# A two-model forward pass on one core: eight swaps in the mixers' list, and another head, hand-over and tail

## The reference

```python
def first_block(x, ...):                      # two blocks
    for l in range(2):
        h = rms_norm(x, norm_mix[l])
        if l == 0: x = x + pool_attn_mixer(h, ...)   # 4 pooled groups and 8 attention heads, then pa_w_out
        else:      x = x + rglru_mixer(h, ...)       # gated linear recurrence, then rg_w_out
        x = x + conv_ffn(rms_norm(x, norm_ffn[l]), ...)
    return x

def second_block(x, c, ...):                  # one block
    sh1, sc1, gt1, sh2, sc2, gt2 = jnp.split(silu(c) @ ada_w[l] + ada_b[l], 6)
    p = (rms_norm_2(x, norm_mix_g[l]) * (1.0 + sc1) + sh1) @ w_in[l]
    y_a = rwkv7_mixer(p[..., :OFF_B], ...)    # the recurrence: state (state*w + sa b + v k) over positions
    y_b = spatial_gating_mixer(...); y_c = short_conv_mixer(...)
    y_d = s5_mixer(p[..., OFF_D:OFF_G], ...)  # complex diagonal state space, scans over positions
    gates = jax.nn.sigmoid(p[..., OFF_G:])
    x = x + gt1 * ((gates[0] * y_a + gates[1] * y_b + gates[2] * y_c + gates[3] * y_d) @ w_o[l])
    x = x + gt2 * (square(relu(h2 @ ffn_w1[l])) @ ffn_w2[l])
    return rms_norm_2(x, final_g)
```

## Time and profile before

| | us |
|---|---|
| median of 3 runs | 1149.91 |
| lowest and highest run | 1147.52, 1151.16 |
| the profiled execution's own time | 1149.63 |
| its span in the trace | 1147.8 |
| TensorE busy in it | 1087.0 |

### The profile page before, as it was taken

The page is one execution under the profiler, slowest core; times in us unless marked ns, Lnnn a source line. Parts: engine busy times, 40 slices in busy tenths (PEclk is TensorE's granted clock), DMA queues, the critical chain, the costliest instruction groups (busy, mean ns, idle before and its releaser), DMA issues.

```text
span 1147.8 us, 21003 instructions
## 1 busy us (share of the span) xinstructions
PE 1087.0 (95%) x8588; PEld 1032.6 (90%) x8588; DVE 835.6 (73%) x1444; ACT 641.7 (56%) x1098; POOL 67.2 (6%) x79
## 2 busy tenths in 40 slices
PE   6996999999998969999999999999999999999996
PEld 6874999999997859999999988899989989999996
DVE  6464898887886387987787778998875587655452
ACT  7544676665565786656555685322233368875340
POOL 1231200000102001000000000000000011000010
PEclk9998999999999979999999999999999999999998
DMA  9366365556665845676776553222335275556651
GB/s 341 116 202 230 132 210 182 185 171 183 190 199 194 276 149 166 214 235 216 239 235 183 191 170 106 88 84 90 121 105 154 70 252 181 184 179 182 182 159 37
DMA packets 59856, 200.41 MB, mean 175 GB/s; under 512 B 6768, under 2 KB 11504, under 8 KB 59632
## 3 DMA queue, kind: packets, MB, share of 16 engines
q1 hardware_dynamic: 58032, 194.54, 52.7%
q10 hardware_dynamic: 1728, 4.53, 1.1%
HBM read 197.99 MB, written 1.05 MB: 173 GB/s over the span
## 4 chain that ended last, share of the span: by engine, by line
PE 81%; DVE 10%; ACT 5%; DMA 2%; issue 1%; ACTq 0%; SPq 0%; POOL 0%; DVEq 0%
PE ps L472 81%; DVE wlo L1556 2%; ACT whi L1039 1%; DVE xr L1562 1%; DMA ring<-pa_w_out 1%; ACT L1039 1%; DMA ring<-pa_w_in 1%; ACT xr L1039 1%; ACT rr L1039 0%; DMA ring<-w_o 0%; DVE rst L1585 0%; DVE raw L1556 0%; DVE bks L1556 0%; DVE hl L1556 0%; ACT sc L1039 0%
## 5 line engine op out<-in xcount | busy, mean ns | idle before, releaser
L472 PE MATMUL ps<-hh,whi 128*128 128x256 f32 (+1 forms) x1656 | 481.2, 291 | 18.0 <-DVE wlo L1556 15.5
L472 PE MATMUL ps<-hh,wlo 128*128 128x256 f32 (+1 forms) x1656 | 471.1, 284 | 0.0
L472 PE MATMUL ps<-hl,whi 128*128 128x256 f32 (+1 forms) x1656 | 469.1, 283 | 0.0
L1556 DVE TENSOR_TENSOR wlo<-ring,whi 128x1024 fp32r<-128x1024 f32 (+1 forms) x313 | 376.1, 1216 | 70.6 <-ACT whi L1039 69.9
L1039 ACT ACTIVATE whi<-ring 128x1024 fp32r<-128x1024 f32 (+1 forms) x313 | 321.7, 1039 | 72.4 <-PE ps L472 52.4
L472 PEld LDWEIGHTS ps<-hh,whi 128*128 128x128 f32 x1656 | 316.2, 191 | 38.8 <-issue 31.0
L472 PEld LDWEIGHTS ps<-hl,whi 128*128 128x128 f32 x1656 | 316.9, 191 | 1.6 <-issue 1.2
L472 PEld LDWEIGHTS ps<-hh,wlo 128*128 128x128 f32 x1656 | 316.4, 191 | 0.0
L472 PE MATMUL ps<-hidh,whi 128*128 128x256 f32 x608 | 172.2, 283 | 0.0
L472 PE MATMUL ps<-hidh,wlo 128*128 128x256 f32 x608 | 172.1, 283 | 0.0
L472 PE MATMUL ps<-hidl,whi 128*128 128x256 f32 x608 | 172.0, 283 | 0.0
(11 more groups left out here) (360 smaller groups left out, 1345.6 us busy)
## 6 DMA issues: line engine op xcount, KB each, us to landing
ring<-ffn_w_in SPq DMA_DIRECT2D x88, 512.0 KB, 4.1
ring<-ffn_w SPq DMA_DIRECT2D x64, 512.0 KB, 4.1
ring<-w_in SPq DMA_DIRECT2D x51, 512.0 KB, 3.4
ring<-ada_w SPq DMA_DIRECT2D x48, 512.0 KB, 4.3
ring<-ffn_w_out SPq DMA_DIRECT2D x32, 448.0 KB, 3.4
ring<-rg_w_in SPq DMA_DIRECT2D x20, 512.0 KB, 4.3
ring<-pa_w_in SPq DMA_DIRECT2D x16, 512.0 KB, 7.4
ring<-ffn_w_out SPq DMA_DIRECT2D x16, 512.0 KB, 3.6
```

What stands on the lines that cost most here:

```text
L472: return e.matmul(o, l, r, start=start, stop=stop)
L1556: return e.tensor_tensor(o, a, b, op)
```

## The change

Four edits stand in it. In the head, ten matmuls of a buffer of zeros are put in front on TensorE, which no longer waits there for the constants; chunk 0 lands and is split in two halves, each with its own signal; the two larger of ACT's three DMAs are issued behind chunk 0. At the end of the attention stage, the eighth A moves to the end of ATTN, its chunks ahead of pa_w_out's, pa_w_out reads its inputs in the order 4, 5, 6, 3, 2, 7, 1, 0, and `mod_turn` is called behind column 2 only. In PLAN, eight pairs "S", "R" become "R", "S". In the tail, four DMAs of two tiles replace eight of one.

```diff
 ATTN = [ ...
-    ("A",), 0, ("T", 7), ("O", 2), ("G", 3), ("A",), ("G", 2), ("A",), ("O", 3), ("G", 1), ("A",), ("G", 0),
+    ("A",), 0, ("T", 7), ("O", 2), ("G", 3), ("A",), ("G", 2), ("A",), ("O", 3), ("G", 1), ("A",), ("G", 0), ("A",),
 ]
@@ weight_order
     for m in range(8):
         whole("pa_w_out", 8, (m,))
-        if m == 1:
-            columns()
@@ PLAN (one of its lines; eight such pairs in all)
-    "R", (0, 0), "S", "R", (1, 0), "R", (2, 0), "S", "R", (0, 3), "R", (1, 3), "R", (2, 3), "R", (3, 3), "R", (4, 3),
+    "R", (0, 0), "R", "S", (1, 0), "R", (2, 0), "R", "S", (0, 3), "R", (1, 3), "R", (2, 3), "R", (3, 3), "R", (4, 3),
@@ tensor_program, linear(..., rows=range(8))
-                    for q in range(n):
+                    for i, q in enumerate(rows[0:n]):
...
-                            low.wait_ge(e, c)
+                            low.wait_ge(e, c if c or q > 3 else "half")
@@ tensor_program, row_stats
                     p = take(("stat", 0))
+                    ones_in.wait_ge(e, "all")
@@ tensor_program, pool_attn
                 def also(m):
-                    mod_turn()
-                    if m == 0:
-                        mod_step()
-                residual(1, "pa_w_out", 8, ..., also)
+                    if m == 2:
+                        mod_turn()
+                residual(1, "pa_w_out", 8, ..., also, (4, 5, 6, 3, 2, 7, 1, 0))
@@ tensor_program, start
-            ones_in.wait_ge(e, "all")
+            at_dve.wait_ge(e, "zeros")
+            for i in range(10):
+                mm(ps[7][:, 0:T], raw[0][:, 0:128], raw[0], True, True)
@@ scalar_program, feed (DVE's feed splits chunk 0 in the same way)
+                        if n == 0:
+                            act(whi[0][:, 0:4, :], ring[0][:, 0:4, :], ACT.Copy).then_inc(*high.up("half"))
+                            landed_late.wait_ge(e, "all")
+                        k = 0 if n else 4
+                        act(whi[j % NS][:, k:nk, :], ring[n % NR][:, k:nk, :], ACT.Copy).then_inc(*high.up(n))
@@ scalar_program, start
-            e.dma_start(cst[:, 0:384], d["cst"][:, 0:384]).then_inc(*ones_in.up("all", 16))
-            e.dma_start(vec[:, 32:], d["vec"][:, 32:]).then_inc(*vecs_in.up("all", 16))
...
                 if m == 3:
                     feed(-1 - AHEAD)
+                    e.dma_start(cst[:, 0:384], d["cst"][:, 0:384]).then_inc(*ones_in.up("all", 16))
+                    e.dma_start(vec[:, 32:], d["vec"][:, 32:]).then_inc(*vecs_in.up("all", 16))
@@ sync_program
+                if n == 0:
+                    e.dma_start(dst[:, 0:4, :], src[:, 0:4, :]).then_inc(*landed[0].up(0, 16))
+                    e.dma_start(dst[:, 4:, :], src[:, 4:, :]).then_inc(*landed_late.up("all", 16))
...
-            for m in range(8):
-                fin.wait_ge(e, m)
-                e.dma_start(out[:, m, :], x[:, m, :]).then_inc(*x_out.up("all", 16))
+            for m in (0, 2, 4, 6):
+                fin.wait_ge(e, m + 1)
+                e.dma_start(out[:, m:m + 2, :], x[:, m:m + 2, :]).then_inc(*x_out.up("all", 16))
```

More of the change, by code:

```diff
@@ L491, in give, with linear @@
                 freed[b] = s, ev
-            def linear(w, ms, of, nk, need):
+            def linear(w, ms, of, nk, need, rows=range(8)):
                 outs = [take((w, m))[:, 0:T] for m in ms]
@@ L500, in linear @@
                         for (c, _, _), o in zip(parts, outs):
-                            low.wait_ge(e, c)
+                            low.wait_ge(e, c if c or q > 3 else "half")
                             j = turn[c] % NS
-                            mm(o, whi[j][:, q, :], rh, k + q == 0, False)
+                            mm(o, whi[j][:, q, :], rh, k + i == 0, False)
                             mm(o, whi[j][:, q, :], rl, False, False)
-                            t = mm(o, wlo[c % NR][:, q, :], rh, False, k + q == nk - 1)
-                            if q == n - 1:
+                            t = mm(o, wlo[c % NR][:, q, :], rh, False, k + i == nk - 1)
+                            if i == n - 1:
                                 t.then_inc(*through.up(c))
@@ L538, in stats, with residual @@
                 give(("stat", n), mean, n)
-            def residual(n, w, nk, of, need, also=None):
+            def residual(n, w, nk, of, need, also=None, rows=range(8)):
                 for ms in ([0, 1], [2], [3], [4], [5], [6], [7]) if nk == 8 else [[m] for m in range(8)]:
-                    linear(w, ms, of, nk, need)
+                    linear(w, ms, of, nk, need, rows)
                     for m in ms:
@@ L679, in also @@
                 def also(m):
-                    mod_turn()
-                    if m == 0:
-                        mod_step()
-                residual(1, "pa_w_out", 8, pair(pah, pal), lambda k: at_dve.wait_ge(e, ("pal", k)), also)
+                    if m == 2:
+                        mod_turn()
+                residual(1, "pa_w_out", 8, pair(pah, pal), lambda k: at_dve.wait_ge(e, ("pal", k)), also, (4, 5, 6, 3, 2, 7, 1, 0))
             def conv_ffn(l):
@@ L1050, in feed @@
                             used(e, at_turn[j - NS])
-                        act(whi[j % NS][:, 0:nk, :], ring[n % NR][:, 0:nk, :], ACT.Copy).then_inc(*high.up(n))
+                        if n == 0:
[3 more added lines that the diff above has]
+                        act(whi[j % NS][:, k:nk, :], ring[n % NR][:, k:nk, :], ACT.Copy).then_inc(*high.up(n))
             def out_of(w, m, nk=8):
@@ L1218, in pool_attn @@
                         part[at[0]](*at[1:])
-                def also(m):
-                    next(steps, None)
-                    if m == 0:
-                        mod_step()
-                residual(1, "pa_w_out", 8, also)
+                residual(1, "pa_w_out", 8, lambda m: next(steps, None))
             def conv_ffn(l):
@@ L1573, in feed @@
                         nk, j = order[n][3], n % NR
+                        if n == 0:
+                            high.wait_ge(e, "half")
+                            low_of(wlo[0][:, 0:4, :], ring[0][:, 0:4, :], whi[0][:, 0:4, :]).then_inc(*low.up("half"))
+                        k = 0 if n else 4
                         high.wait_ge(e, n)
-                        low_of(wlo[j][:, 0:nk, :], ring[j][:, 0:nk, :], whi[turn[n] % NS][:, 0:nk, :]).then_inc(*low.up(n))
+                        low_of(wlo[j][:, k:nk, :], ring[j][:, k:nk, :], whi[turn[n] % NS][:, k:nk, :]).then_inc(*low.up(n))
             def out_of(w, m, nk=8):
@@ L2306, in vector_program @@
             e.memset(dmy[:, :], 1.0).then_inc(*at_dve.up("dummy"))
+            e.memset(raw[0], 0.0).then_inc(*at_dve.up("zeros"))
             gains_in.wait_ge(e, "all")
```

8 lines of the change are left out of this document (5 added, 3 removed), and 6 rows, old and new, of the table PLAN.

## The result

The changed kernel takes 1141.06 us (median of five runs, 1135.94 to 1143.30), the kernel before 1149.91 in runs beside it: ratio 0.9918, 95% interval 0.9891 to 0.9945. It is 8.9 us faster, where 13.6 were forecast. The profiled execution of the changed kernel is its slowest, 1143.30, with a span of 1141.5; the one of before had 1147.8, so 6.3 us lie between the two traces.

The account below looks back on a forecast made before the run. TensorE, busy 1087.0 of 1147.8 us, was taken to bound the kernel, with some 61 us of waits. 9.9 + 1.2 + 2.1 + 0.4 = 13.6 us gave a median of 1136.3, range 1131.5 to 1142.5 (8 in 10).

Parts of the forecast that it names:

- The end of the attention stage: Around pa_w_out: shorter wait before it, none before mrow's transposes, less low clock; -9.9 us, bounds 11.6 and about 7.
- can only act on waits: Whole kernel: real matmuls stay the same in number, so only waits, the clock behind them and the ends can change.
- The low stretch of 1.7 us: Behind the 2.3 us wait left at pa_w_out: one stretch at low clock kept, costing 1.7 us.
- The mixers: The eight swaps in PLAN: the 2.10 us wait for aald goes; -2.1 us, bounds 0 and 2.3.
- Priced at nothing: Mixers: R's matmuls moved ahead of S5's two products delay S5's block by at most 2.4 us, counted as no cost.
- The term for the seventh swap: Mixers, S9 with R24: ve,at comes first on TensorE, aald is done sooner, and the 2.10 us wait goes.
- S5's next step, a column or more later: Mixers: this, with chunks converted five ahead, was said to cover the later start of S5's block; cost nothing.
- the swaps do nothing: Rival, mixers: DVE is late at R24 anyway or the recurrence waits again later; 2.1 us missing, 1138.4 us; chance 0.08.
- The head: Start of the kernel: row_stats at 17.5 instead of 19.59, part lost to low clock; -1.2 us, bounds 0 and 2.1.
- The tail: Output DMAs: four issues keep pace with DVE, so the last starts sooner; -0.4 us, bounds 0 and 0.6.
- Conversion takes the place of the input: Rival, pa_w_out: ACT's stop at chunk 1 lasts to 99, TensorE waits 4.9 us as before; 1138.9 us; chance 0.09.
- Every gap costs clock: Rival, head and attention end: each wait left brings a low stretch of 1.7 us; 11.1 us gained, 1138.8; chance 0.16.

Follow-up runs that it names:

- x7: Changed kernel, but pa_w_out reads its inputs from 0 to 7 again; 1141.74 us, ratio 0.9940.
- y2: x2_one_swap with the eight steps of S5's parameters moved from pa_w_out into columns 8 to 15 of the first ffn_w_in; 1134.15 us, ratio 0.9864.
- x5: Changed kernel with the eight steps of S5's parameters moved from pa_w_out into the first ffn_w_out, two a column; 1143.51 us, ratio 0.9939.
- x2_one_swap: Changed kernel with only the seventh swap (S9 with R24) kept, the other seven undone; 1133.22 us, ratio 0.9857.
- y3_old_head: Changed kernel with the whole head of before; 1139.10 us, ratio 0.9917.
- x3_split_swap: Changed kernel with only the seventh swap, taken by ACT and DVE; TensorE walks the list of before; 1135.14 us, ratio 0.9872.
- x4_no_zeros: Changed kernel without the ten matmuls of zeros in front; 1136.96 us, ratio 0.9904.

## Why the prediction was right in its direction, with a gain 4.7 us too large

**The end of the attention stage, -9.9 forecast, about 8.2 in the traces (8.8 up to 320 less the 0.5 of the head): the mechanism held, one cost was missing.** The wait at pa_w_out fell to 0.98 us instead of 2.3 (chunk 1 was converted from 95.25 to 96.31; I had it end at 97.5), the wait before mrow is gone, and the clock is high there. That is 8.4 us of waits where 7.1 were forecast. What failed is the step behind the sentence that the change "can only act on waits": I took the waits of before and priced pa_w_out's columns by TensorE alone, so that no new wait could appear. DVE was at 5.8 and 5.9 of 6 us in the last four of these columns before the change too, just covered. TensorE is through with them at 124.4 instead of 136.9 and meets it: 2.12 us and a low stretch came back at the eighth column. x7 and y2 show this from two sides; x5 shows less, because its wait at pa_w_out is longer by 1.7 us.

Luck hid part of this miss. The forecast has 2.3 us of waits in all where the nine traces have 2.15 to 3.18, and the changed kernel's 3.10; it has them in one place, and they come in two. The low stretch of 1.7 us that I put behind pa_w_out's wait was never there (none of 12 traces); one of the same size came behind stats, in this trace alone. Of the 1.7 us between 9.9 and 8.2, 0.8 are the longer waits; the rest is not accounted for.

**The mixers, -2.1 forecast, no gain measured (176.4 to 176.9 us of the stretch against 175.8 and 176.3): the sum failed in "Priced at nothing".** The term for the seventh swap was right (2.10 forecast, 1.9 to 2.4 by x2_one_swap). The others cost 2.7 us. The cover that I named, "S5's next step, a column or more later", holds for S5's data. Not looked at was what S5's work releases: a PSUM bank for the recurrence's next product, and DVE's time ahead of `ve`. The rival "the swaps do nothing" had the number right, for another reason than it named.

**The head, -1.2 forecast, 0.5 in the traces: the start of row_stats came as said (17.41 for 17.5), with the gap before it; the clock took most of it.** I took the middle between no low stretch and one of 1.7 us; where one comes it takes up to 3.4 us (6.8 us at half speed), and it comes in two of three traces that wait there. Against y3_old_head the new head gains 0.9 us at full clock, which is no more than the scatter of the means, and loses 1.7 to the low clock. **The tail**, -0.4, is as measured.

**The rivals.** "Conversion takes the place of the input" did not come: the wait is 0.98 us. "Every gap costs clock" gave 1138.8. The Trainium skill, TensorE: Matmul & The Clock Gate, section "HAM oscillation — how this bites in real kernels", tells of a kernel in which the wait for data throttles the clock each time; the waits that it draws are 3 to 5 us, longer than those left here, so it bears less on this rival than the prediction made of it. In the traces a low stretch follows some waits and not others: that of 2.73 us for wlo (at 390 to 405) in 13 of 14, that of 2.3 us for xr (344 to 358) in 8 of 14, the head's 1.8 us in 6 of 9, the 0.7 to 2.1 us before stats in 1 of 9, the 0.9 to 2.7 us at pa_w_out in none of 12. At pa_w_out it does follow the two longer waits, 4.08 us in x7 and 4.95 before; yet a wait of 3.27 us for ScalarE's `gvT` (six traces) is never followed by one. So the rival is right that gaps cost clock, and wrong in "every". The profiled execution had bad luck on top: the low stretch at 922.60 took 2.2 us more, and only three of the fourteen traces have one there.

The balance of the profiled executions: 8.8 (head and hand-over, up to 320), less 0.5 in the mixers, less 2.2 at 922, plus 0.4 in the tail, is 6.5, where the spans differ by 6.3. Over all runs the full-clock part fell by 4.2 us and the part that the low clock takes by 4.8. The two steps that failed can be put right in the kernel: x2_one_swap has 3.1 us less at full clock than the changed kernel, and y2_params_mid another 1.8.

## What to carry to other kernels

When a large wait is removed, look for the engine that is next in the stretch behind it, by windows of a few us: work that TensorE's wait had covered (here VectorE is 0.1 to 0.4 us a column slower than TensorE) becomes the wait. Judge the new wait together with the one ahead of it, since they trade. When one list moves ahead of another, price what the later one releases, PSUM banks above all, not only its data; and move only the step whose wait the trace shows. Where the clock falls by chance, compare span x clock over several runs, and don't judge a change of 2 us by one trace.

## What was not expected of the hardware

Many waits repeat to some hundredths of a us from trace to trace (1.45, 1.08, 2.3, 2.73, 1.99 us at the same instructions); the clock behind them does not. The two waits around pa_w_out are the exception. The wait for xr and the window of 4 us behind it, first in x3_split_swap, then in x2_one_swap:

```profile
344.09 0.67 PE L478 MATMUL ps<-xr,wab 128*128 128x256 f32 x2 [2.35 <-DVE xr L1570]
```

```profile
344.10:348.10 4.00, 4.00 (x16) 2.30 (x16) 1.32 (x3) 2.16 (x5) 0.91 (x2) 0.57 0.08 32
```

```profile
347.26 0.67 PE L470 MATMUL ps<-xr,wab 128*128 128x256 f32 x2 [2.31 <-DVE xr L1562]
```

```profile
347.20:351.20 4.00, 3.94 (x24) 2.64 (x25) 1.81 (x4) 3.23 (x6) 1.46 (x2) 1.00 0.12 47
```

To the next wait of 2.73 us it is 47.05 us in the one (391.14 - 344.09) and 45.45 in the other (392.71 - 347.26): that low stretch costs 1.6 us. Another costs nothing. The wait for ve and the one behind it, in the changed kernel (the clock is low from 704.7 to 708.1; 0.88 in the mean between the two) and in x4_no_zeros (1.00):

```profile
704.64 1.22 PE L470 MATMUL ps<-ve,cst 128*128 128x512 f32 x1 [1.99 <-DVE ve L1562]
719.39 0.84 PE L470 MATMUL ps<-ws,gvT 128*64 128x128 f32 x11 [1.66 <-ACT gvT L1040]
```

```profile
700.48 0.70 PE L470 MATMUL ps<-ve,cst 128*128 128x512 f32 x1 [2.00 <-DVE ve L1560]
715.23 1.01 PE L470 MATMUL ps<-ws,gvT 128*64 128x128 f32 x14 [3.27 <-ACT gvT L1038]
```

Both take 14.75 us from wait to wait: at the low clock TensorE is 1.6 us longer at work and waits 1.6 us less for ScalarE. In all fourteen traces the second wait is 1.7 us where the clock was low (eight) and 3.3 where it was not (six). And in nine of them the clock is low for 3.4 us between 48 and 56 with no wait of over 0.5 us in the 10 us before; what sets that one stays open.
